# Three Strassen pairs in the down product of the conv FFN, on one Trainium2 core

## What is computed

```
h    = rms_norm_2(x, ffn_norm)
u    = h @ ffn_w_up                      # 1024 -> 2 * 3072
u    = causal_depthwise_conv(u, w, b)    # 3 taps along the tokens
gate, up = split(u)
x    = x + (gelu(gate) * up) @ ffn_w_down   # 3072 -> 1024
```

## Time and profile before

| what | value |
|---|---|
| median of 3 runs | 2938.76 us (2938.32 to 2939.37) |
| span of the profiled execution, first to last instruction | 2937.1 us |
| instructions | 40238 |
| TensorE busy | 2919.6 us, 14312 matmuls |
| weight loads of TensorE busy | 2388.5 us |
| VectorE, ScalarE, GpSimd busy | 1309.0, 1288.6, 1322.3 us |
| mean granted TensorE clock | 0.999 |

### The profile page before, as it was taken

The page is one execution under the profiler, slowest core; times in us unless marked ns, Lnnn a source line. Parts: engine busy times, 40 slices in busy tenths (PEclk is TensorE's granted clock), DMA queues, the critical chain, the costliest instruction groups (busy, mean ns, idle before and its releaser), DMA issues.

```text
span 2937.1 us, 40238 instructions
## 1 busy us (share of the span) xinstructions
PE 2919.6 (99%) x14312; PEld 2388.5 (81%) x14312; DVE 1309.0 (45%) x2190; ACT 1288.6 (44%) x2017; POOL 1322.3 (45%) x743
## 2 busy tenths in 40 slices
PE   9999999999999999999999999999999999999999
PEld 7888888888878888888888877778888887888887
DVE  5657534221063667434222076654554138455510
ACT  4556545322253556444223265554444228444421
POOL 4454355444434554455444443444444443444443
PEclk9999999999999999999999999999999999999999
DMA  4222232323322232333333322212333322233333
GB/s 145 73 87 80 81 122 92 99 94 100 108 86 87 73 98 68 94 115 106 94 99 101 108 80 71 61 56 94 98 95 98 95 94 94 93 100 93 100 104 90
DMA packets 77275, 273.37 MB, mean 93 GB/s; under 512 B 8776, under 2 KB 9416, under 8 KB 77152
## 3 DMA queue, kind: packets, MB, share of 16 engines
q1 hardware_dynamic: 74112, 266.05, 29.0%
q10 hardware_dynamic: 3040, 5.64, 0.6%
HBM read 269.55 MB, written 2.10 MB: 92 GB/s over the span
## 4 chain that ended last, share of the span: by engine, by line
PE 93%; DVE 2%; ACT 2%; POOL 1%; issue 1%; DMA 0%; SPq 0%; DVEq 0%; ACTq 0%; POOLq 0%
PE ps L822 25%; PE ps L824 25%; PE ps L823 25%; PE ps L1122 2%; PE ps L1153 2%; PE ps L1100 2%; PE ps L1375 2%; PE ps L1381 1%; PE ps L1376 1%; PE ps L1226 1%; PE ps L1232 1%; PE ps L1227 1%; ACT WHI L1534 1%; PE ps L1095 1%; PE ps L1097 0%
## 5 line engine op out<-in xcount | busy, mean ns | idle before, releaser
L2894 POOL TENSOR_TENSOR WLO<-WRAW,WHI 128x1024 fp32r<-128x1024 f32 x393 | 949.8, 2419 | 1158.5 <-ACT WHI L1534 1158.2
L822 PE MATMUL ps<-HH,WHI 128*128 128x512 f32 x2144 | 842.1, 393 | 2.4 <-POOL WLO L2894 0.9
L824 PE MATMUL ps<-HH,WLO 128*128 128x512 f32 x2144 | 834.8, 389 | 0.0
L823 PE MATMUL ps<-HL,WHI 128*128 128x512 f32 x2144 | 834.4, 389 | 0.0
L1534 ACT ACTIVATE WHI<-WRAW 128x1024 fp32r<-128x1024 f32 x467 | 490.6, 1051 | 281.6 <-DMA WRAW<-wall 280.8
L822 PEld LDWEIGHTS ps<-HH,WHI 128*128 128x128 f32 x2144 | 402.5, 188 | 91.2 <-issue 5.3
L824 PEld LDWEIGHTS ps<-HH,WLO 128*128 128x128 f32 x2144 | 402.4, 188 | 84.7
L823 PEld LDWEIGHTS ps<-HL,WHI 128*128 128x128 f32 x2144 | 402.7, 188 | 81.1
L2746 DVE SCALAR_TENSOR_TENSOR ps<-U,COLS,ps 128x512 f32<-128x512 f32 x192 | 145.0, 755 | 122.6 <-ACT ps L1993 108.5
L2228 DVE TENSOR_TENSOR ACC<-ACC,SQ 128x512 f32<-128x512 f32 x78 | 68.4, 877 | 280.5 <-ACT SQ L1819 271.1
L2980 POOL TENSOR_SCALAR SG<-SG,RS 128x512 f32<-128x512 f32 (+3 forms) x104 | 109.9, 1067 | 141.1 <-DVE RS L2508 141.1
(11 more groups left out here) (422 smaller groups left out, 4805.4 us busy)
## 6 DMA issues: line engine op xcount, KB each, us to landing
WRAW<-wall SPq DMA_DIRECT2D x502, 512.0 KB, 3.5
y<-X ACTq DMA_DIRECT2D x8, 256.0 KB, 4.0
X<-xin SPq DMA_DIRECT2D x3, 512.0 KB, 7.9
DFT<-dft ACTq DMA_DIRECT2D x4, 258.0 KB, 4.3
PT_IN<-pin ACTq DMA_DIRECT2D x2, 512.0 KB, 3.7
DIL<-dil ACTq DMA_DIRECT2D x1, 768.0 KB, 4.6
X<-xin SPq DMA_DIRECT2D x2, 256.0 KB, 4.7
COLS<-cols ACTq DMA_DIRECT2D x1, 290.5 KB, 5.3
```

The lines of the kernel that those rows point to most:

```text
L822: pe.matmul(out_, WHI[w_at], x_hi, start=first, stop=False)
L823: pe.matmul(out_, WHI[w_at], x_lo, start=False, stop=False)
L824: return pe.matmul(out_, WLO[w_at], x_hi, start=False, stop=last)
L2894: pool.tensor_tensor(WLO[:, s, :], whole, WHI[:, s, :].bitcast(F32), ALU.subtract).then_inc(wt_lo, 1)
```

## The change

The down product is moved into the up product and six of its eight output tiles are made by Strassen's scheme in the Winograd form.

- The 24 hidden tiles are made in three chunks (`CHUNKS`). A chunk is an up stage of four repetitions (16 units, 8 hidden tiles), followed by a `down` stage of eight units that adds the chunk's share to `X`. Each FFN has three such pairs of stages, so the kernel has six down stages.
- In a down stage the first and the last unit are direct: output tiles 0 and 7, with 8 input tiles and 24 matmuls of 512 columns each. Between them stand three pairs of output tiles, each with two units (`pair_order`). A paired unit holds, for two pairs of input tiles, the four blocks A12, A11, A22 and A21 of weights; TensorE makes seven products of 128 x 128 by 256 columns for each pair of input tiles, each again as three matmuls: 42 matmuls per unit. The matmuls of input tile 7 of the first direct unit are held back until the first paired unit is done, and `unit_used` then counts both.
- Four sums of weight blocks are made per paired unit: on GpSimd for the first pair's units (four additions of 256 elements per partition), on VectorE for the other four (`sums_of`, four reductions that read 2, 2, 3 and 4 blocks). They go to `XRAW`, and are split into `XHI` and `XLO` like weights; of the slot itself three blocks (768 elements) are split.
- The forms of the activations (`mixed`) are made on VectorE at the end of each repetition in `TM`, three operations, and split as two more rows (ScalarE 1024 elements, VectorE 1024 elements).
- The seven products of a pair stand in four PSUM banks. When a pair's second unit is done ScalarE copies the first product to `TM`, and VectorE puts the results together and adds them to `X` in seven operations, each with at most one SBUF input (`pair_added`).
- The loops of the up stages are written out.

```diff
+CHUNKS = ((0, 4), (4, 4), (8, 4))
+KEPT = 3 * 2 * P
+PRODUCTS = ((0, "slot", A11, B11), (2, "slot", A12, B21), (1, "extra", R2, T2), (3, "extra", R4, B22),
+            (4, "slot", A22, T4), (5, "extra", R1, T1), (6, "extra", R3, T3))
...
+        for k0, m in CHUNKS:
...
+            up = add("conv_ffn", m, 4, 4, {"conv_begun": 4, "conv_tap_added": 8, "gate_ready": 2, "product_ready": 2, "operand_hi_ready": 3, "operand_ready": 3, "mixed": 3},
...
+            add("down", 1, PAIRS * m // 2 + 2, 8, per, made=up, heads=PAIRS, last=last, gain=gain)
...
+            def down(st):
+                up, order = st.made, order_of(st)
...
+                weights(st.unit(0))
+                pe.wait_ge(bank_free[st.bank(0)], st.use(0))
+                direct(0, 0, range(kt - 1))
+                for j, p, b in paired_steps(st):
+                    if p == 1 and b == 0:
+                        pe.wait_ge(bank_free[st.bank(0)], st.use(4))
...
+                    if p == 2 and b == 0:
+                        pe.wait_ge(S["pair_step"], st.at("pair_step", PAIR_STEPS))
+                    weights(st.unit(j))
...
+                        for h, home, block_, x in PRODUCTS:
...
+                            pe.matmul(o, w_hi, FTH[:, row, cols_], start=first, stop=False, skip_group_check=True)
+                            pe.matmul(o, w_hi, FTL[:, row, cols_], start=False, stop=False, skip_group_check=True)
+                            mm = pe.matmul(o, w_lo, FTH[:, row, cols_], start=False, stop=last, skip_group_check=True)
+                    if j == 1:
+                        direct(0, 0, range(kt - 1, kt)).then_inc(unit_used, 2)
+                    else:
+                        mm.then_inc(unit_used, 1)
+                j = len(order) - 1
+                weights(st.unit(j))
+                pe.wait_ge(bank_free[st.bank(3)], st.use(7))
+                direct(j, 3, range(kt)).then_inc(unit_used, 1)
...
+            def split_paired(n):
...
+                act.activation(WHI[:, s, 0:KEPT], WRAW[:, s, 0:KEPT], ACT.Copy).then_inc(slot_hi, 1)
+                act.wait_ge(*sums_ready(n))
+                act.activation(XHI[:, e, :], XRAW[:, e, :], ACT.Copy).then_inc(wt_hi, 1)
...
+                    p = ended_at(st, j)
+                    if p is not None:
+                        act.wait_ge(unit_used, st.unit(j) + 1)
...
+                        act.activation(TM[:, 0, 0:HALF], ps[pair_bank(p, 0)][:, 0:HALF], ACT.Copy).then_inc(S["first_copied"], 1)
...
+            def sums_of(st, j, r=0):
+
+                n = st.unit(j, r) + AHEAD
+                if n not in SUMS["vector"]:
+                    return
+                s, e = n % SLOTS, PAIRED[n] % EXTRA
+                w = WRAW[:, s, :].rearrange("p (b c) -> p c b", c=2 * P)
+                dve.wait_ge(raw[s], 16 * (n // SLOTS + 1))
+                for i, blocks in ((R1, slice(A22, A21 + 1)), (R3, slice(A11, A21 + 1, 2)), (R2, slice(A11, A21 + 1)), (R4, slice(A12, A21 + 1))):
+                    dve.tensor_reduce(sum_of(e, i), w[:, :, blocks], AXX, ALU.add).then_inc(summed["vector"], 1)
...
+            def mixed(st, r, b, at):
...
+                dve.tensor_tensor(t[:, 0:2, :], b[:, b12:b12 + 1, :].to_broadcast([P, 2, HALF]), b[:, b11:b22 + 1:b22 - b11, :], ALU.subtract)\
...
+                dve.tensor_tensor(t[:, 2, :], t[:, 1, :], b[:, b11, :], ALU.subtract).then_inc(S["mixed"], 1)
...
+                dve.tensor_tensor(t[:, 3, :], b[:, b21, :], t[:, 2, :], ALU.add).then_inc(S["mixed"], 1)
...
+            def pair_added(st, p):
...
+                dve.wait_ge(S["first_copied"], st.at("first_copied", p + 1))
+                step(dve.tensor_tensor(t[:, 3, :], t[:, 0, :], bank[0][:, HALF:SEQ], ALU.add))
+                wait(1)
+                step(dve.tensor_tensor(t[:, 1, :], t[:, 3, :], bank[2][:, HALF:SEQ], ALU.subtract))
+                step(dve.tensor_tensor(t[:, 2, :], t[:, 3, :], bank[3][:, 0:HALF], ALU.subtract))
+                wait(2)
+                step(dve.tensor_tensor(bank[1][:, :], bank[1][:, :], TM[:, 0, :], ALU.add))
+                wait(3)
+                step(dve.tensor_tensor(both, both, t[:, 2:3, :].to_broadcast([P, 2, HALF]), ALU.subtract))
+                wait(4)
+                step(dve.tensor_tensor(x[0], x[0], bank[1][:, :], ALU.add))
+                wait(5)
+                step(dve.tensor_tensor(x[1], x[1], bank[2][:, :], ALU.add))
...
+            def down(st):
+                for j in range(st.units):
+                    p = ended_at(st, j - 1)
+                    if j == 2:
+                        direct_added(st, 0, 0, 0)
+                    if p is not None:
+                        pair_added(st, p)
+                    sums_of(st, j)
...
+                direct_added(st, DT - 1, st.units - 1, 3)
...
+            def remainder_paired(n):
...
+                    pool.tensor_tensor(sum_of(e, R1), a[A22], a[A21], ALU.add).then_inc(summed["pool"], 1)
+                    pool.tensor_tensor(sum_of(e, R3), a[A11], a[A21], ALU.add).then_inc(summed["pool"], 1)
...
+                    pool.tensor_tensor(sum_of(e, R2), sum_of(e, R3), a[A22], ALU.add).then_inc(summed["pool"], 1)
...
+                    pool.tensor_tensor(sum_of(e, R4), sum_of(e, R2), a[A12], ALU.add).then_inc(summed["pool"], 1)
+                pool.wait_ge(*sums_ready(n))
+                pool.wait_ge(slot_hi, PAIRED[n] + 1)
+                pool.tensor_tensor(WLO[:, s, 0:KEPT], WRAW[:, s, 0:KEPT], WHI[:, s, 0:KEPT].bitcast(F32), ALU.subtract)
+                pool.wait_ge(wt_hi, n + 1)
+                pool.tensor_tensor(XLO[:, e, :], XRAW[:, e, :], XHI[:, e, :].bitcast(F32), ALU.subtract).then_inc(wt_lo, 1)
```

More of the change, by code:

```diff
@@ L124, with pair_order @@
 COL, N_COLS = column_plan()
+def pair_order(pairs, blocks):
+    return [None] + [(p, b) for p in range(pairs) for b in range(blocks)] + [None]
 def unit_list():
@@ L195 @@
 FOLDS = {n: f for f, n in enumerate(FOLD_UNITS)}
+PAIRED = {n: q for q, n in enumerate(n for n, unit in enumerate(UNITS) if unit[0].endswith(" paired"))}
+SUMS = {who: {n: q for q, n in enumerate(n for n in PAIRED if (UNITS[n][4] == P) == (who == "pool"))} for who in ("pool", "vector")}
 HOSTS = ("fourier_branch", "branch_mla")
@@ L769, in first_of, with halves, mixed_rows, order_of @@
             return st.made is not None and st.made.kind == "init"
+        def halves(x):
+            return x.rearrange("p a s -> p (a s)").rearrange("p (n c) -> p n c", c=HALF)
+        def mixed_rows(r):
+            return FTH[:, 4 * r + 2:4 * r + 4, :], FTL[:, 4 * r + 2:4 * r + 4, :]
+        def order_of(st):
+            return pair_order(st.heads, st.made.reps // 2)
+        def ended_at(st, j):
+            last = st.made.reps // 2 - 1
+            return next((p for i, p, b in paired_steps(st) if i == j and b == last), None)
+        def paired_steps(st):
+            return [(j, *unit) for j, unit in enumerate(order_of(st)) if unit is not None]
+        def tiles_done(st, j):
+            if j == 1:
+                return (0,)
+            p = ended_at(st, j)
+            return () if p is None else (1 + 2 * p, 2 + 2 * p)
+        def pair_bank(p, b):
+            return 4 * (1 - p % 2) + b
+        def sums_ready(n):
+            who = "pool" if n in SUMS["pool"] else "vector"
+            return summed[who], 4 * (SUMS[who][n] + 1)
+        def sum_of(e, i):
+            return XRAW[:, e, i * 2 * P:(i + 1) * 2 * P]
         def gate_at(n):
@@ L1299, in body @@
                 def body(r):
-                    if isinstance(r, int) and r == 0:
+                    if isinstance(r, int) and r == 0 and st.norm is not None:
                         (opening_fast if st.kind == "conv_ffn" else opening_slow)(st)
@@ new lines, in direct_added, with down @@
+            def direct_added(st, t, j, k):
+                dve.wait_ge(unit_used, st.unit(j) + 1)
+                dve.tensor_tensor(X[:, t, :], X[:, t, :], ps[st.bank(k)][:, :], ALU.add).then_inc(S["direct_added"], 1)
+                dve.engine_nop().then_inc(bank_free[st.bank(k)], 1)
+            def down(st):
+                for j in range(st.units):
+                    p = ended_at(st, j - 1)
[4 more added lines that the diff above has]
+                    sums_of(st, j)
+                    if st.last and j:
+                        for t in tiles_done(st, j - 1):
+                            finished(st, t)
+                direct_added(st, DT - 1, st.units - 1, 3)
+                if st.last:
+                    finished(st, DT - 1)
@@ L2768, in recurrent, with finished @@
+            def finished(st, t):
+                if st.gain:
+                    remainder(st, (HH[:, t, :], HL[:, t, :]), X[:, t, :], t + 1, 0, col(st.gain, t))
+                    dve.wait_ge(S["square_ready"], st.at("square_ready", t + 1))
+                    add_square(st, t, 0, t % 2)
             def recurrent(st):
@@ L2888, in remainder_of @@
                 s = n % SLOTS
```

(3 more changed lines are left out.)

149 lines of the change are left out of this document (125 added, 24 removed).

## The result

The kernel with the change takes 2984.56 us (2983.8 to 2985.95, 4 runs) against 2938.6 us (2938.32 to 2939.37, 4 runs) before: ratio 1.0156, 95% interval 1.0142 to 1.017. It is 46 us slower. The forecast was 24 us slower, 2963 us, with 2944 to 3015 us as the range for 8 in 10. The sign was right, and so were the stalls before the third and the fourth unit of a stage; the forecast rise was about half of the measured one.

A forecast was written before the change was run, and what follows sets the result against it. TensorE's matmul stream was taken to bound the kernel, preparation hidden. Six down stages at +3.9 us (+23.6) plus 1 us for the norm gave span 2961.7; with runs' median 1.7 us above span, 2963 us, range 2944 to 3015.

The forecast's parts named there:

- the stalls before the third and the fourth unit of a stage: Down stages: TensorE idle 2.1 us before unit 2 and 3.6 us before unit 3.
- TensorE's saving: Conv FFNs: 256-column matmuls 0.120 us apart, 7.2 us less per FFN, 14.4 us in all; 41.1 us a stage against 43.52.
- Blocking by GpSimd: Each chunk's last repetition: two-SBUF-input VectorE operations wait for GpSimd; mixed-forms remainder ends at 13.7, unit 2 stalls 2.1 us.
- Unit 3: Down stage: weights ready at 21.3, direct addition done at 20.9, TensorE free at 17.7; stall 3.6 us.
- Unit 6: Down stage: sums behind the first pair's additions, weights at 37.0 when due at 36.4; stall 0.6 us.
- The sums: VectorE's four reductions per unit at the row's rate, 0.69 + 0.69 + 0.95 + 1.22, less overlap 3.3 us.
- Rival A: VectorE's reductions run slowly from hops, at the scan's price: 6.2 us a unit, stage 59.4, 3034 us; chance 0.22.
- the 5.2 us estimated from the page for a unit's sums: VectorE's sums at the skill page's 1.73 ns per element: 5.2 us a unit, 55.2 us a stage, 3009 us.
- The norm's work: Last chunk of the FFN before a norm: squares and gain copies fall among the sums, adding 1 us.
- B: Down stages: blocking is mild because operations interleave; units 1 and 2 pass unstalled, stage 44.8, 2947 us; chance 0.12.
- C: Down stages: preparation hidden, all stalls of a stage below 2.4 us, TensorE's saving stands, 2924 us; chance 0.07.
- D: Down stages: something between B and C, within the bound; chance 0.07.

The follow-up runs named there:

- experiment 10: Changed kernel with direct addition earlier, unit 3's sums before the last mixed-forms remainder, norm work later, VectorE's sums replaced by one fill (not the full computation): 2937.76 us, 0.9994.
- experiment 2: Changed kernel with VectorE's fourth sum made as the R2 sum plus block A12, one 256-element addition, instead of a four-block reduction: 2974.53 us, 1.0122.
- experiment 7: Kernel before the change with 36 test operations appended on VectorE, mostly reductions of 2, 3 or 4 values at several distances, nothing beside them: 2987.4 us.
- experiment 8: Changed kernel with VectorE's four sums per unit replaced by one fill of 1024 elements (output not the product), GpSimd's sums kept: 2945.2 us, 1.0021.
- Experiment 5: Changed kernel with the norm's squares and gain copies moved: tiles 0 to 2 after the second pair, 3 to 6 after the third: 2982.7 us, 1.0147.
- experiment 4: Changed kernel with VectorE making unit 3's sums before the remainder of the last repetition's mixed forms: 2976.3 us, 1.0129.
- experiment 3: Changed kernel with idle matmuls of ones keeping TensorE busy ahead of the wait for unit 3: 2988.42 us, 1.017.
- experiment 1: Changed kernel with VectorE's direct addition of tile 0 moved ahead of the sums of unit 4: 2984.48 us, 1.0156.
- experiment 11: Version of experiment 6 with VectorE's sums made by three plain additions (512, 256, 256 elements) instead of reductions: 2960.7 us, 1.0073.
- experiment 6: Changed kernel with the edits of experiments 1, 2, 4 and 5 together: 2952.12 us, 1.0045.

## Why the prediction was right in sign and wrong in size

- **TensorE's saving: right.** The 256-column matmuls stand 0.120 us apart in the units that nothing slows (5.04 us a unit), and experiment 10, with one late start of 0.7 us left, gives 42.1 us: 41.1 plus that and 0.3.
- **Blocking by GpSimd: right, a little too strong.** The remainder of the mixed forms was held up until it took 3.3 us, and ended at 12.2, not 13.7; unit 2's stall was 0.7, not 2.1.
- **Unit 3: right in place and size, for two errors that cancel.** Forecast 21.3, with the direct addition at 20.9 and GpSimd's weights at 21.3; measured 20.84 and 20.5. The early end of the remainder made up for slower sums.
- **Unit 6: right by coincidence.** The forecast had a wait of 0.6 us, because its weights would come at 37.0. They came at 38.3, but TensorE was as late itself, from the clock after unit 3's stall, and waited 0.2 us in one normal stage alone.
- **The sums: the step that failed first.** "I take the lower, because the instruction is the same and only the addresses differ." The addresses matter once four blocks are read: 1.97 us in the kernel, 1.885 alone, against 1.22. Over the sums of four units that is 3.0 us, less the 1.5 by which the remainder of the mixed forms ended early, which leaves 1.5. Measured is 1.3: unit 6's weights come at 38.3 instead of 37.0, and the stage is 49.0 to 49.2 instead of 47.5. Six times about 1.6 is 9 to 10 us of the 22 that were missing. Experiments 2, 7 and 8 show it from three sides. Not all of it would have gone with the forecast's price: in experiment 2, where the reduction over four blocks is gone, the clock alone keeps half of the stages at 48.1 to 48.3. Rival A had the mechanism, but it charged every element with the scan's price; two and three blocks ran at the full rate or near it. The stage it gave (59.4) did not come.
  The Trainium skill's figure for a source that hops on every element (page "Vector Engine (DVE) Microarchitecture Reference", "Measured stream behaviour on trn2") is 1.73 ns. Measured here are, after 0.16 us of fixed time, 1.69 ns for four values, but 1.04 and 1.14 for two and three: the trace agrees with the rule for four values and, for two, with the exception that the page notes; three lie near the full rate, and the 5.2 us estimated from the page for a unit's sums were 4.15.
- **The norm's work: the step that failed most.** "I add 1 us for one more blocked operation or two." The stage lost 9.7 us more than the others and the way behind it 4.7. Its operations stand in VectorE's list ahead of the very sums and additions that TensorE waits for, in a stage where that list was already full. Seven tiles bring 14 of them, and the four that GpSimd held up took 2.9 us each instead of 0.7. I had counted them as work in a gap, when they were work in the binding chain. That is 13.4 us of the 22. Experiment 5 shows it, and also that little of it can be had back by a move, since the norm must open the next FFN. The two steps that failed are not independent: with VectorE's sums left out (experiment 8) the norm stage is only 6.2 us longer than the others and the way behind it only 0.8 longer than before the change, 7.0 us in place of 14.4.
- **The clock: not foreseen.** It made the stages of experiments 2 and 4 vary by 1.2 and 1.6 us. In the changed kernel it came out level with unit 6's late weights, so that either alone would have given nearly the same stage (experiment 3 for the clock taken away).
- **Rivals B, C and D: refuted as forecast.** B failed because the blocking was not mild (an operation of 1.22 us took 3.3). C named the right condition, though: with the lists rearranged and nearly free sums the preparation is hidden. Even then 7.5 us go behind the norm stage, and the time is level with before.

Experiments 1 and 3 tell the same thing from two ends: unit 3 is released by VectorE's addition and by GpSimd's weights within 0.4 us of each other, and unit 6 stands behind both, so taking away one of them gains nothing. The single gains of experiments 2, 4, 5 and 1 sum to 20 us; together they give 32.

## What to carry to other kernels

Trading TensorE's time for helpers' time pays only if each helper's list, written in order with what GpSimd blocks, ends before each unit is due: here a saving of 2.4 us a stage stood against a VectorE list that ran for 25 us with one pause of 1.4, so work put into that list (a norm's squares, one slow reduction) moved the end of the stage. Find the gate behind the gate before you remove a stall, and test the helpers' bound by leaving their work out in the rearranged version. Where GpSimd is busy most of the time, as here, count short VectorE operations with two SBUF inputs at two to three times their free price (experiment 11: 1.43, 1.32 and 0.94 us against 0.69, 0.43 and 0.43). That made three short additions (3.7 us, 1.5 when free) dearer than three reductions and one addition (3.4 us, 2.8 when free).

## What the hardware showed that was not expected

- A reduction over four blocks runs at 1.69 ns an element at each of the six distances tried between 256 and 1024 elements; over two blocks it runs at 1.04 and over three at 1.14 (256 and 512 elements apart), over four adjacent values at 1.04 (experiment 7, after 0.16 us of fixed time).
- After 4.5 us without a matmul the granted clock of the next 7.7 us was 0.61, spacing 0.21 us instead of 0.12; after 1.4 us (experiment 6) the unit behind the wait had 1.00. In between it went either way: after about 2.1 us before unit 6 in experiment 4 the clock of the unit was 0.74 in one stage and 1.00 in the next, and after 1.8 us in the norm stage of experiment 8 it was 0.74.
- GpSimd's remainders also get longer where VectorE's operations with two SBUF inputs stand beside them: 2.83 us instead of 1.85 and 2.84 instead of 2.40 (the rows of experiment 10 and of the changed kernel).
